# Modulation sums of the later blocks: 32x32 squares turned and added on VectorE, one folding product on TensorE

## The reference, cut to what matters

```
mod = silu(c) @ w_mod[i] + b_mod[i]            # 1024 -> 6144
sh1, sc1, g1, sh2, sc2, g2 = split(mod, 6)
x = x + g1 * mixer(norm(x) * (1 + sc1) + sh1)
x = x + g2 * swiglu(norm(x) * (1 + sc2) + sh2)
```

## Time and profile before

| | us |
|---|---|
| median of 3 runs | 2128.09 |
| lowest and highest run | 2118.55, 2129.23 |
| the profiled execution, whole | 2124.51 |
| its span, first to last instruction | 2122.4 |
| TensorE busy, share of the span | 95% |
| VectorE busy, share of the span | 47% |
| mean granted TensorE clock | 0.967 of 2.4 GHz |

### The profile page before, as it was taken

How to read it: one execution, slowest core, us unless ns; L and a number is a source line. 1 busy time by engine, 2 the same in 40 slices (tenths; PEclk the granted TensorE clock), 3 DMA queues, 4 the chain that set the end, 5 groups by cost and what they waited for, 6 DMA issues and landing times.

```text
span 2122.4 us, 28746 instructions
## 1 busy us (share of the span) xinstructions
PE 2017.7 (95%) x12081; PEld 1742.5 (82%) x12081; DVE 992.6 (47%) x1875; ACT 601.7 (28%) x1101; POOL 74.3 (4%) x121
## 2 busy tenths in 40 slices
PE   7879999988899999999998999998989999999998
PEld 2768888767788888888887788888878888888887
DVE  1877425684766665652235334544452222222224
ACT  3235224652321112211223333334232211211213
POOL 2010000000011101100000000000000000000000
PEclk9889999999899999999998999999989999999999
DMA  7343112012344444432223201021212222222212
GB/s 282 120 150 108 41 41 80 21 31 60 99 142 138 136 122 139 142 96 60 65 62 104 60 20 41 21 99 49 61 50 60 60 70 60 64 66 60 62 56 82
DMA packets 210249, 174.16 MB, mean 82 GB/s; under 512 B 10320, under 2 KB 196792, under 8 KB 208584
## 3 DMA queue, kind: packets, MB, share of 16 engines
q1 hardware_dynamic: 197536, 117.67, 18.5%
q0 software_dynamic: 12288, 48.35, 7.1%
q10 hardware_dynamic: 296, 6.29, 0.7%
HBM read 162.85 MB, written 9.44 MB: 81 GB/s over the span
## 4 chain that ended last, share of the span: by engine, by line
PE 87%; DVE 6%; ACT 4%; issue 2%; DMA 1%; POOL 0%; ACTq 0%; DVEq 0%; POOLq 0%
PE bank L824 60%; PE bank L790 9%; PE bank L842 4%; PE bank L1096 2%; PE bank L747 1%; PE bank L765 1%; DMA early_raw<-in_w_mod_dram 1%; ACT w_hi L1221 1%; DVE early_acc L1620 1%; DVE w_lo L1601 1%; PE bank L1018 1%; PE bank L908 1%; PE bank L1041 1%; PE bank L966 1%; PE bank L1068 1%
## 5 line engine op out<-in xcount | busy, mean ns | idle before, releaser
L824 PE MATMUL bank<-h_hi,w_hi 128*128 128x256 f32 x1600 | 409.4, 338 | 0.1
L824 PE MATMUL bank<-h_lo,w_hi 128*128 128x256 f32 x1600 | 407.5, 336 | 0.0
L824 PE MATMUL bank<-h_hi,w_lo 128*128 128x256 f32 x1600 | 407.3, 336 | 0.0
L1601 DVE TENSOR_TENSOR w_lo<-raw,w_hi 128x1024 fp32r<-128x1024 f32 (+4 forms) x195 | 239.0, 1230 | 340.2 <-ACT w_hi L1221 340.1
L824 PEld LDWEIGHTS bank<-h_hi,w_lo 128*128 128x128 f32 x1600 | 301.3, 188 | 33.6
L824 PEld LDWEIGHTS bank<-h_lo,w_hi 128*128 128x128 f32 x1600 | 301.4, 188 | 33.2
L824 PEld LDWEIGHTS bank<-h_hi,w_hi 128*128 128x128 f32 x1600 | 299.4, 188 | 34.2 <-issue 1.9
L1221 ACT ACTIVATE w_hi<-raw 128x1024 fp32r<-128x1024 f32 (+4 forms) x196 | 205.6, 1053 | 226.3 <-DMA raw<-in_ffn_w_down_dram 129.1
L790 PE MATMUL bank<-w_hi,h_hi 128*128 128x256 f32 x672 | 214.8, 320 | 18.1 <-DVE w_lo L1601 17.7
L790 PE MATMUL bank<-w_lo,h_hi 128*128 128x256 f32 x672 | 195.8, 291 | 0.0
L790 PE MATMUL bank<-w_hi,h_lo 128*128 128x256 f32 x672 | 195.6, 291 | 0.0
(11 more groups left out here) (274 smaller groups left out, 2251.7 us busy)
## 6 DMA issues: line engine op xcount, KB each, us to landing
raw<-in_ffn_w_gu_dram SPq DMA_DIRECT2D x176, 256.0 KB, 3.3
late_raw<-in_w_mod_dram POOLq DMA_DIRECT2D x56, 512.0 KB, 4.3
raw<-in_ffn_w_down_dram SPq DMA_DIRECT2D x64, 256.0 KB, 3.3
early_raw<-in_w_mod_dram POOLq DMA_DIRECT2D x24, 512.0 KB, 4.4
wide<-in_w_mod_dram SPq DMA_DIRECT2D x8, 1024.0 KB, 18.7
raw<-in_odd_w_in_dram SPq DMA_DIRECT2D x16, 512.0 KB, 4.4
raw<-in_even_w_in_dram SPq DMA_DIRECT2D x24, 256.0 KB, 5.0
x_kept<-x ACTq DMA_DIRECT2D x2, 3072.0 KB, 10.3
```

Of the source, the lines that this page charges most:

```text
L824: last = mm(pair(u.pair)[s], wk[a], seq(operand(o, k), s), start=(k == 0 and n == 0), stop=(k == u.ks - 1 and n == 2))
L1601: v.tensor_tensor(lo, r, hi.bitcast(F32), ALU.subtract).then_inc(unit_split, 1)
```

## The change

For blocks 6 to 19 the sum over partitions is begun on VectorE. Behind the last part of a block, `sum_blocks` turns the block's 128 x 1024 accumulators in 32x32 squares into `turned_acc` and adds them up along rows of 32, which leaves 128 x 32 partial sums (`block_sums`, two buffers): four partial sums of each column, in four groups of 32 partitions. On TensorE one product per block remains: a 128 x 128 matrix `fold`, four by four identity matrices of 32 x 32, is stationary, and the 32 columns of partial sums move through it. It writes 32 columns of bank 7, where every group of 32 partitions then holds all sums. `complete` picks from it, for each group of 32 partitions, every fourth column: eight additions of 32 x 4 in place of two of 128 x 4. `fold` is made on GpSimd at the start (one memset, four selects), behind the issue of the constants' loads. TensorE waits for two semaphores more at each of these sums. Blocks 0 to 5 stay as they were.

```diff
+        turned_acc = at("turned_acc", Z + 86 * KB, [P, 2 * MOD_BLOCK])
+        block_sums = own("block_sums", [P, 2, 2, MOD_BLOCK // 32])
+        fold = own("fold", [P, P])
...
+        N_EARLY = EARLY // MOD_PARTS
+        def fold_bank(b):
+            return bank[7][:, 256 + b % 2 * 32:256 + (b % 2 + 1) * 32]
...
             for dst, src in consts:
                 pool.dma_start(dst, src).then_inc(consts_loaded, 16)
+            nc.gpsimd.memset(fold[:], 0.0).then_inc(fold_ready, 1)
+            pool.wait_ge(fold_ready, 1)
+            nc.gpsimd.affine_select(out=fold[:].rearrange("p (a b) -> p a b", b=32), in_=fold[:].rearrange("p (a b) -> p a b", b=32),
+                                    compare_op=ALU.not_equal, fill=1.0, base=0, pattern=[[0, 4], [-1, 32]], channel_multiplier=1
+                                    ).then_inc(fold_ready, 1)
+            for g in range(1, 4):
...
                 pe.wait_ge(mod_ready, b + 1)
+                if b >= N_EARLY:
+                    pe.wait_ge(fold_ready, 5)
+                    pe.wait_ge(sums_ready, b - N_EARLY + 1)
+                    mm(fold_bank(b), fold[:], block_sums[:, b % 2, :, :].rearrange("p s c -> p (s c)"), start=True, stop=True
+                       ).then_inc(mod_full, 1)
+                    return
                 for m in range(MOD_BLOCK // P):
...
+            def sum_blocks(b):
+                for s in range(2):
+                    dve.wait_ge(acc_step[s], KD * (b + 1))
+                link(v.transpose(turned_acc[:], mod_acc(b).rearrange("p s c -> p (s c)")))
+                v.tensor_reduce(block_sums[:, b % 2, :, :].rearrange("p s c -> p (s c)"),
+                                turned_acc[:].rearrange("p (c i) -> p c i", i=32), AX.X, ALU.add).then_inc(sums_ready, 1)
             def complete(n, l, c0, c1):
...
                 for s in range(2):
-                    last = v.tensor_tensor(mod[l][:, c0:c1, s], columns[:, c0:c1, s], b_cols[:, l * MODT + c0:l * MODT + c1], ALU.add)
+                    if n > N_EARLY:
+                        sums = fold_bank(n - 1).rearrange("p (s c q) -> p s c q", s=2, q=4)
+                        for q in range(4):
+                            r = slice(32 * q, 32 * q + 32)
+                            last = v.tensor_tensor(mod[l][r, c0:c1, s], sums[r, s, :, q], b_cols[r, l * MODT + c0:l * MODT + c1], ALU.add)
+                    else:
+                        last = v.tensor_tensor(mod[l][:, c0:c1, s], columns[:, c0:c1, s], b_cols[:, l * MODT + c0:l * MODT + c1], ALU.add)
...
                             modulate(m)
+                            if m >= EARLY and m % MOD_PARTS == MOD_PARTS - 1:
+                                sum_blocks(m // MOD_PARTS)
```

More of the change, by code:

```diff
@@ L285, in build @@
         row_taken = sem("row_taken")
+        fold_ready = sem("fold_ready")
+        sums_ready = sem("sums_ready")
         hi_ready = sem("hi_ready")
@@ L677, in _ @@
                 pool.dma_start(dst, src).then_inc(consts_loaded, 16)
+            nc.gpsimd.memset(fold[:], 0.0).then_inc(fold_ready, 1)
[4 more added lines that the diff above has]
+            for g in range(1, 4):
+                pool.wait_ge(fold_ready, g + 1)
+                nc.gpsimd.affine_select(out=fold[:].rearrange("p (a b) -> p a b", b=32), in_=fold[:].rearrange("p (a b) -> p a b", b=32),
+                                        compare_op=ALU.not_equal, fill=1.0, base=-32 * g, pattern=[[0, 4], [-1, 32]], channel_multiplier=1
+                                        ).then_inc(fold_ready, 1)
             tri = [junk[:, 0:P], junk[:, P:2 * P]]
```

## The result

| | before | changed |
|---|---|---|
| median, us | 2125.24 (4 runs, one more than above) | 2104.74 (4 runs) |
| lowest and highest | 2118.55, 2129.23 | 2102.65, 2108.84 |
| the profiled execution, its span | 2124.51, 2122.4 | 2104.56, 2102.4 |

The ratio is 0.9913 [0.9884, 0.9942]. The forecast was 2105 (2096 to 2114).

The account below looks back on a forecast made before the run. TensorE was taken as the bound (87% of the chain of waits, VectorE 6%). 2124.5 - 20.9 + 0.1 = 2103.7 us, or 2107.3 against the median; it said 2105 us, range 2096 to 2114.

Parts of the forecast that it names:

- What TensorE loses: Late sums on TensorE: 1.70 us becomes 0.21 per block, saving 20.9 us over 14 blocks, bounds 17.8 to 23.8.
- The first rival: The fold on TensorE costs more than its passes, 0.32 us more per sum, 4.5 in all: 2109 us; chance 0.08.
- the rival that the sums were hidden: TensorE's late sums were hidden anyway, so nothing changes: 2124 us; chance 0.02.
- VectorE's new work: Turning and summing each late block: about 2.5 us, bounds 1.7 and 4.8; with the longer `complete`, 3.6 us per block.
- the price without overlap: `complete` on VectorE: eight additions at 0.17 us each without overlap, 1.36 us, 1.14 more than now.
- The rival that VectorE is hot: Turning and summing take 4.8 us and delays carry into the next units: 2116 us; chance 0.07.
- the slower one: VectorE's pair takes longer than a sum's room, break-even at 11 us, at 13 us TensorE loses 28: 2132 us; chance 0.03.
- the loads: GpSimd's next load of a part waits for VectorE's steps and is no later than VectorE is: cost nothing.
- the end of gu00: New work fits VectorE's 2.59 us idle ahead of `prod` with 0.1 to spare: cost 0.1 us, bounds 0 and 2.3.
- the hole: Sign of being right: TensorE's hole at the end of gu00 is still 1.2 to 1.4 us.
- the stretch of the sums: Sign of being right: the stage from the first late sum to the last is shorter by 19 to 21 us.
- GpSimd: Making `fold` at the start, four selects and a memset, 1.4 us: costs nothing, with 47 us of cover before `band_i` is used.

Follow-up runs that it names:

- e3: Changed kernel without VectorE's turning and summing (partial sums are zeros written once), TensorE's single product per late block kept: 2098.39 us, 0.9878 of the kernel before.
- e8: Changed kernel with turning and summing moved behind the take of the unit on VectorE's queue: 2099.86 us in one run.
- e2: Changed kernel with VectorE's turning and summing done but unread, TensorE's eight products per block and the two old additions kept: 2124.29 us, 1.0004 of before.
- e6: Changed kernel with turning and summing done four times for each late block: 2166.54 us in one run.
- e1: The changed kernel run again with no edit: 2104.09 us, 0.9909 of the kernel before.
- e11: Changed kernel with both the next pair of banks for the first down unit and turning and summing behind the take: 2102.2 us, 0.9875 of before.
- e7: Changed kernel with blocks 0 to 5 also summed the new way, VectorE waiting for x to be stored: 2113.93 us, 0.9952 of before.
- e4: Changed kernel with the first down unit of a group going on to the next pair of banks: 2092.39 us, 0.9872 of before.
- e9: Kernel before, without the change, with only the first down unit moved to the next pair of banks: 2115.42 us, 0.9943 of before.
- e10: Changed kernel with the next pair of banks for the first down unit, and 512 columns ahead of 256 in each pair: 2105.6 us, 0.9889 of before.
- e5: Changed kernel with turning and summing done twice for each late block: 2106.66 us, 0.9919 of before.

## Why the prediction held, point by point

**What TensorE loses.** Saved per block 1.70 - 0.14 = 1.56 us, forecast 1.49 (bounds 1.27 and 1.70); for 14 blocks 21.8 against 20.9. A fold took 0.14 us, not two passes of 0.106: this product alone between two streams cost less than I allowed, not more. e3 and e8 show the 21.8 in the stretch. The first rival, a fold that costs more than its passes, and the rival that the sums were hidden are refuted by this.

**VectorE's new work.** Turning 1.245 and summing 1.220 us, 2.5 with the wait: the split's price, as taken. `complete`'s eight additions take 1.36 us, which is the price without overlap.

```profile
670.93 1.36 DVE L1669 TENSOR_TENSOR mod<-bank,b_cols 32x4 f32<-32x4 f32 x8
```

The Trainium skill's rule that an instruction in another group of 32 partitions waits for all earlier ones ("VectorE: DVE Perf Modes", "Two Vector instructions with no wait between them") agrees with it. The advice of the Trainium skill against the sum along rows as the slowest operation ("VectorE: DVE Perf Modes", "Rules for kernel authors") is not borne out here: 1.220 us is no more than the split's 1.222 over as many elements, and e2 and e8 show the work hidden.

VectorE is busy for 295.9 of 379 us, 78%, forecast 79%. TensorE never waited for `block_sums`; the smallest room was 4.4 us at block 15, as 6.97 - 2.5 has it. The rival that VectorE is hot, and the slower one, did not happen. The slower one's own arithmetic was wrong, though: it put the break-even at a pair of 11 us, and e6, with four pairs or some 10 us, was already 43 us slower than before. I had looked at rooms alone and not at VectorE's sum of work. Its 2132 us is a slip as well: 28 us is already the loss net of the saving, so it stands for about 2152, on top of the 2124.5.

**The step that failed** is the loads ("it is late by what VectorE is late, which is no more. Cost: nothing"), and with it the 0.1 us for the end of gu00. The hole cost 1.57 there (2.27 in e1), inside its bound of 2.3; with the clock behind it 3.1, which is outside. Two of the prediction's own signs came out against it: the hole, to be 1.2 to 1.4 us, is 2.72, and the stretch of the sums, to be 19 to 21 us shorter, is 17.0 (18.8 in e1). VectorE in order of time, changed kernel, against the earlier trace rows:

```profile
680.21 2.74 DVE L1647 SCALAR_TENSOR_TENSOR late_acc<-late_raw,c_cols,late_acc 128x512 f32<-128x512 f32 x4 [1.37 <-DMA late_raw<-in_w_mod_dram]
683.06 1.25 DVE L1656 STREAM_TRANSPOSE turned_acc<-late_acc 128x1024 f32<-128x1024 f32 x1
684.34 1.22 DVE L1657 TENSOR_REDUCE block_sums<-turned_acc 128x32 f32<-128x1024 f32 x1
685.59 1.02 DVE L1800 TENSOR_TENSOR prod<-silu_g,bank 128x256 f32<-128x256 f32 x2
```

The accumulation waited 1.37 us for its load and ended at 682.95, 1.04 us ahead of TensorE's end at 683.99, where it had been 2.59 ahead. Two passes of 2.5 us don't fit in 1.04: `prod` comes 1.56 late, which is the wider hole. Without the load's wait it would have ended at 681.58, 2.41 ahead, and 0.1 to 0.2 us would have been left over, about as forecast. The load's row on GpSimd says why it is late: it waited for VectorE to be through with the part two before it.

```profile
675.63 0.72 POOL L730 DMA_DIRECT2D late_raw<-in_w_mod_dram  x1 [10.78 <-DVE late_acc L1647]
```

The load took 4.6 us from issue to landing, where before it took 4.2 (5.0 in e1 and e3): it did not get shorter with the rest. Before, it was issued 10.88 us ahead of TensorE's end of gu00, and now 8.36 (683.99 - 675.63):

```profile
676.63 0.72 POOL L709 DMA_DIRECT2D late_raw<-in_w_mod_dram  x1 [9.36 <-DVE late_acc L1620]
```

Since the `prod` that opens this pass of VectorE, TensorE has one sum less to do (1.54), and VectorE has 1.14 us more of `complete`, which together are about the difference. The idle time ahead of the split, 2.36 us before, which the prediction set against the longer `complete`, is gone: the split at 677.63 follows the accumulation at once, and the wait has moved behind it, to the load. e3 has the wait without the turning, e2 the turning without the wait; only both together cost. That part is shown. How much of the load's lateness is `complete`'s and how much TensorE's is worked out from the rows and was not tried apart, and no run has the load earlier with all else as changed.

**Not in the prediction at all:** the clock's fall behind the hole (1.57 us) and the two spacings of the large products (1.7 us inside the stretch). Behind the stretch, 4.0 us came back where the change does nothing: from the last large product of layer 0's feed-forward to the first behind layer 1's mixer are 359.2 us in place of 363.3. The thirteen profiles, of all kernels here, lie between 356.6 and 363.3 in it, so this belongs to the single execution. That the total came within 1 us of the forecast is luck in this sense: what the hole, the clock and the spacing took is about what the mixer and a fold cheaper than priced gave back. The mechanism and its size are confirmed by the stretches of e3, e8 and e11, not by the total.

**GpSimd** cost nothing, as forecast, at 2.0 us in place of 1.4: four selects of 0.30 us and a memset at 6.6 to 8.6 us. `band_i` starts 1.95 us later, at 10.84, and is used at 57.0, where it was at 56.8.

## What to carry to other kernels

Work moved from a full engine to one with idle time pays nearly its whole length, as long as the receiving engine's sum of work stays under the stage (doubling the new work cost 2.6 us by the medians, quadrupling it 62) and nobody waits for that engine there (in e7's early stage others did, and 9.5 us were lost though VectorE was not full); but run the clock forward at each place where the full engine waits for the other one, since a load of fixed length that was early may come last once everything ahead of it is sooner. A hole that the profile calls issue may be a PSUM bank that is freed late, and behind a hole that had grown the granted clock fell in most of the profiles here. Giving the next group another bank closed all four holes (e4, 0.9872): faster than the kernel before; its median is 11.7 us under the changed kernel's, though the two intervals overlap.

## What was not expected of the hardware

**Large products run at two spacings at a full granted clock.** A pair of 256 and 512 columns takes 346.7 or 353.3 ns (the longer in a pattern of some 358, 356 and 346), nearly always unchanged from one hole in TensorE's work to the next. In the changed kernel's profile gu00 has the longer, the last group of gu of the layer the shorter. The table by stretch gives the granted clock 1.00 for both, which is 2.4 GHz, and 343 records in 60 us (four of them passes of folds) against 549 in 95: 176 and 173 ns for one.

```profile
600.00:660.00 60.00, 60.00 (x343) 52.06 (x342) 48.16 (x75) 14.12 (x20) 6.51 (x10) 1.00 0.48 144
960.00:1055.00 95.00, 95.00 (x549) 83.77 (x549) 23.51 (x27) 19.46 (x28) 0.00 (x0) 1.00 0.21 63
```

The difference is 1.9%, some 10 us if all of a layer's 530 us of feed-forward go one way. It appears with the change (e1), without it (e9) and with either order of the widths (e10). What sets it stays open, and so does how much of the spread of one kernel's runs, 10 us and more, it makes: only the profiled executions can be read for it.

**The granted clock fell behind a hole of under 3 us.** Behind gu00 the granted clock fell to about a half, the lower level of 1.2 GHz, for some 3.5 us in the changed kernel (hole of 2.72 us), to 0.59 on average over the first 2.5 us in e7 (3.67), and for longer in e5 (5.90), and stayed at 1.00 in e1 (3.43). In before, e2, e3 and e8, with holes of 1.16 us, it stayed at 1.00. So behind the wider holes it fell in most executions and not in all; the fall cost 1.57 us in the changed kernel and in e7, and 2.73 in e5. What decides it in one execution was not found.

**A short product between two streams cost little.** Two passes of 32 columns delayed the stream by 0.14 us, while 16 passes of one column took 1.70, 0.106 each.
